# Scores of the gated linear attention by eight levels of block widths, its output mixed tile by tile

## The chip, the cores and the metric

The kernel is one program on one core of a Trainium2 chip. The metric is the device time of one execution in microseconds (us). TensorE (PE) multiplies, and loads its weights beside that (PEld); VectorE (DVE), ScalarE (ACT) and GpSimd (POOL) work elementwise; SyncE (SP) issues the DMAs. PE's clock is granted at one of two levels, 2.4 or 1.2 GHz; the views give it as 1.00 or 0.50.

## The reference

Two decoder layers over 256 positions of width 1024, in float32. Layer 0 is a mix of attention heads and a dense SwiGLU, layer 1 a gated linear attention (GLA) and a mixture of eight experts. The change lies in the GLA:

```python
def gla_mixer(h, w_in, w_a2, b_a, o_norm, w_out):
    q, k, v, r, a1 = _split(h @ w_in, C_SPLITS)          # 4 heads, dk 128, dv 256
    q = q.reshape(B, S, H, dk) * (dk ** -0.5)
    log_a = (jax.nn.log_sigmoid((a1 @ w_a2 + b_a).astype(jnp.float32)) / GLA_TAU).reshape(B, S, H, dk)
    ...
        b = jnp.cumsum(gc, axis=2)
        o_inter = jnp.einsum('bhcd,bhde->bhce', qc * jnp.exp(b), state)
        decay = jnp.where(causal, jnp.exp(jnp.where(causal, dlt, 0.0)), 0.0)   # dlt = b_i - b_j
        att = jnp.einsum('bhid,bhjd,bhijd->bhij', qc, kc, decay)
        o_intra = jnp.einsum('bhij,bhje->bhie', att, vc)
    ...
    o = rmsnorm(o, o_norm).astype(h.dtype).reshape(B, S, GLA_DV) * jax.nn.silu(r)
    return o @ w_out
```

So the score of query i and key j is a sum over 128 channels of q, k and the product of the decays from j+1 to i.

## The kernel before

Activations stand in two tiles of 128 positions (`t`), transposed in `hT_hi` and `hT_lo` (each f32 value as a rounded part and a rest, hence three matmuls per product, `mm3`, L502 to L504). Weights come in a stream of units of 128x2048 (1 MB). SP fetches unit u into one of six `raw` slots once DVE has made the rest of unit u-6. ACT rounds a unit (`split`, L1060: it waits until PE has used unit u-3, `units_used`), DVE makes the rest (L1345), and PE waits for that (`w_lo`). No scheduler is at work: the order of every engine is the order of the code in its block, and semaphores tie the blocks together. Each engine runs its own instructions strictly in that order.

The GLA's stage, from some 372 us to 535 us of the span. The input projection has six column groups `cg` of 8 blocks, two units each: q (0), k (1), v (2, 3) and the output gate r (4, 5).

- PE: `channels(0)` makes q transposed (channels on partitions); L825 makes the decays' logits z; `channels(1)` k; `group` 2, 3, 4; `diagonal(0)` (L840), `group` 5, `cross(0)` (L852, L855), eight dummy matmuls (`keep_busy`), `cross(1)`, `diagonal(1)`, the keys of tile 0 for queries of tile 1 (`far`, L872), the mix of the values (L882, L885), the transposes of the normed output, and the output projection `C_OUT`, tile by tile (`by_tile`), with the second tile's transposes after four blocks of the first tile.
- The scores within a tile come in three kinds. Pairs in one block of 8: DVE makes for each of the 8 offsets the difference of the cumulated logs (L1717), q times k (L1721) and, after ACT's exp (L1197), their product (L1732), and `diagonal` sums over the channels with 8 matmuls of 512 columns against a selecting matrix. Pairs in other blocks of 8 or 32: six copies of k and two of q scaled to block edges (L1694 to L1704, L1775), taken by `cross` in 24 matmuls of 32 or 24 columns per tile. `take_att` (L1740 to L1750) adds the parts, masked, into `att`.
- After the mix, ACT sums squares (L1228), POOL takes the root (L469), DVE multiplies root, output and gate (L1805, `mixed`); the norm's gain was multiplied into the gate before (L1798). `turned` fills `hT_hi` (ACT) and `hT_lo` (DVE) from the transposes; for the output projection it needs no gain, so two instructions per tile and engine (L1069, L1356), while norms with gains take eight (L1075, L1363).

Of the kernel before, what the change touches and what calls it, by code (L numbers as in the profile page):

```python
# [36 lines left out]
P = 128  # L37
# [13 lines left out]
UB = 4  # L51
# [8 lines left out]
GB = 8  # L60
GE = 32
NGE = P // GE
NED = NGE - 1 + GE // GB - 1

# [18 lines left out]
C_ID, C_TRI, C_ONES, C_IOTA, C_BD = 0, 128, 256, 384, 512  # L83
C_BE = 640
C_SEL = 768
C_ROPE = C_SEL + GB + P
# [8 lines left out]
R_QN, R_KN, R_FQ, R_FK, R_ON, R_GB, R_FB = 0, 64, 128, 192, 256, 512, 536  # L95
R_NORM = 544
# [7 lines left out]
def constants():  # L104
# [7 lines left out]
    c[:, C_BD:C_BD + P] = (i[:, None] <= i[None, :]) & (i[:, None] // GB == i[None, :] // GB)  # L112
    c[:, C_BE:C_BE + P] = i[:, None] // GE == i[None, :] // GE

    c[:, C_SEL:C_SEL + GB + P] = np.arange(GB + P)[None, :] % GB == 0
# [37 lines left out]
def trunk(nc, x_d, w_d, const_d, mask_d, small_d, comp_d, wa2_d, out_d):  # L153
    ctx = ExitStack()
    with ctx:
# [49 lines left out]
        mbd = cst[:, C_BD:C_BD + P]  # L205
        mbe = cst[:, C_BE:C_BE + P]
# [51 lines left out]
        gb = cg_(NT * 512).rearrange("p (t n) -> p t n", t=NT)  # L258
        gv = hn
        prod = cg_(GB * 512).rearrange("p (s n) -> p s n", s=GB)  # L260
        kt = cg_(NED * NT * 512).rearrange("p (i t n) -> p i t n", i=NED, t=NT)
        qt = cg_(2 * NT * 512).rearrange("p (i t n) -> p i t n", i=2, t=NT)
        a1T = cg_(SEQ)

        roots, root_diag = esc[:, 0, 0:SEQ], esc[:, 1, 0:SEQ]

        att, atmp = kt[:, 0, :, :], kt[:, 1, :, :]
        gr = kt[:, 2:4, :, :].rearrange("p i t n -> p (i t n)").rearrange("p (t n) -> p t n", t=NT)
        kbar, qbar, far = kt[:, 4, 0, :], kt[:, 5, 0, :], kt[:, 5, 1, :]

        def q_view(i):

            return qt[:, i, :, :].rearrange("p t n -> p (t n)")\
                .rearrange("p (g b r) -> p g b r", b=4, r=(GE, GB)[i])[:, :, 1:4, :]

        def before_edge(a_, i):

            block_, width = (P, (i + 1) * GE) if i < NGE - 1 else (GE, (i - NGE + 2) * GB)
            return a_.rearrange("p (g n) -> p g n", n=block_)[:, :, 0:width]

        def k_view(i):
            return before_edge(kt[:, i, :, :].rearrange("p t n -> p (t n)"), i)


        gz = prod[:, 0:2, :].rearrange("p s n -> p (s n)")
        ge = prod[:, 2:4, :].rearrange("p s n -> p (s n)")
        rmask = prod[:, 4:6, :].rearrange("p s n -> p (s n)")


# [15 lines left out]
        def cf(n):  # L305
# [27 lines left out]
            h2T a1 a1_sb z zb absz soft decay gla_qk gla_vr prod_zero kt_zero diag_arg diag_exp prod diag  # L333
            k_arg k_exp kt q_arg q_exp qt cross att far_arg far_exp far_ops far_psum far_sb gla_o gla_ss
# [5 lines left out]
        def turned_before(g):  # L340

            return sum(NT * NK if j in GAINED else NT * 2 for j in range(g))

# [113 lines left out]
        def _(pool):  # L457
# [26 lines left out]
            pool.wait_ge(S["x_ready"], 4)  # L484
            nc.gpsimd.memset(kt, 0.0).then_inc(S["kt_zero"], 1)
            norm(1)
            norm(2)
            pool.wait_ge(S["decay"], 1)
            nc.gpsimd.memset(prod, 0.0).then_inc(S["prod_zero"], 1)
# [7 lines left out]
        def _(pe):  # L497
# [307 lines left out]

            def channels(cg, b0):

                for k in range(NK):
                    b = cg * NK + k
                    if b == UB:  # L810
                        spread_roots()
                    if b % UB == 0:
                        pe.wait_ge(S["w_lo"], U_C_IN + b // UB + 1)
# [8 lines left out]
            channels(0, 0)  # L822
            pe.wait_ge(S["a1_sb"], 1)
            for h in range(GH):
                last = mm(bank[4 + h // 2][:, h % 2 * SEQ:(h % 2 + 1) * SEQ], wa2[:, h * P:(h + 1) * P], a1T[0:32, :],  # L825
                          start=True, stop=True)
            last.then_inc(S["z"], 1)
            pe.wait_ge(S["zb"], 1)
            channels(1, 4)
            pe.wait_ge(S["gla_qk"], 4)  # L830
            group(U_C_IN, 2, (0, 1))
            group(U_C_IN, 3, (2, 3))
            pe.wait_ge(S["gla_qk"], 8)
            group(U_C_IN, 4, (4, 5))

            def diagonal(t):

                pe.wait_ge(S["prod"], GB * (t + 1))
                for s_ in range(GB):
                    last = mm(bank[t][:, :], cst[:, C_SEL + GB - s_:C_SEL + GB - s_ + P], prod[:, s_, :],  # L840
                              start=(s_ == 0), stop=(s_ == GB - 1))
                last.then_inc(S["diag"], 1)

            def cross(t):
                if t:
                    pe.wait_ge(S["att"], t)
                for h in range(GH):
                    hs = slice(h * P, (h + 1) * P)

                    for i in range(1, NGE):  # L850
                        at = h * P + i * GE
                        mm(bank[2][:, at:at + GE], kt[:, i - 1, t, hs], qt[:, 0, t, at:at + GE], start=True, stop=True)  # L852
# [7 lines left out]

            pe.wait_ge(S["gla_vr"], 4)
            diagonal(0)
            group(U_C_IN, 5, (6, 7))
            pe.wait_ge(S["kt"], 1)
            pe.wait_ge(S["qt"], 1)
            cross(0)
# [1216 lines left out]
```

## Time and profile before

| | us |
|---|---|
| median of 3 runs (lowest, highest) | 1327.59 (1326.4, 1331.55) |
| the profiled execution | 1329.8 |
| its span | 1328.0 |
| PE, DVE, ACT busy in the span | 1288.3, 1036.7, 822.1 |
| the experts' stage, 535 us to the end | 793 |
| the GLA's stage, 372 us to 535 us | 163 |

The last column of a line in the windows is what the DMAs moved; PEclk is the mean granted clock of PE. The chain of work that ended last is followed back from the last instruction, step by step, to what released it: time in it is time that the end depends on. A matmul of float32 data shows as two records.

### The profile page before, as it was taken

How to read it: one execution, taken by the hardware profiler on the slowest of the kernel's cores; microseconds unless marked ns; L12 is line 12 of the kernel's file. 1: busy time of each engine (PE TensorE's matmuls, PEld its weight loads, DVE VectorE, ACT ScalarE, POOL GpSimd, SP SyncE). 2: the span in 40 equal slices, each digit the busy share in tenths (PEclk: the TensorE clock that was granted, in tenths of full speed). 3: DMA queues.
4: the chain of work that ended last, by engine and by line, in shares of the span. 5: the costliest groups of instructions: out<-in, count | busy, mean ns of one | idle time of the engine just before them, and what ended most of it. 6: DMA issues, size and time to landing. Idle time of an engine off the chain costs nothing.

```text
span 1328.0 us, 17323 instructions
## 1 busy us (share of the span) xinstructions
PE 1288.3 (97%) x6142; PEld 1058.1 (80%) x6152; DVE 1036.7 (78%) x1046; ACT 822.1 (62%) x895; POOL 33.1 (2%) x29
## 2 busy tenths in 40 slices
PE   6999999999999999999999999999999999999997
PEld 5877888888888766788888888888888888888885
DVE  4786664455468846789989989989989989989985
ACT  6435364444454535677777777777777777777773
POOL 0130010000001010000000000000000000000000
PEclk9999999999989989999999999999999999999999
DMA  9640045454434302699999989989999999999991
GB/s 375 240 142 18 1 164 188 187 185 185 181 148 158 127 32 95 257 350 366 359 341 362 364 337 366 353 341 363 355 343 360 353 342 356 355 347 372 349 373 74
DMA packets 48793, 350.72 MB, mean 264 GB/s; under 512 B 5424, under 2 KB 5552, under 8 KB 6480
## 3 DMA queue, kind: packets, MB, share of 16 engines
q1 hardware_dynamic: 48720, 349.67, 69.9%
q8 instruction: 55, 0.90, 0.3%
q14 instruction: 18, 0.15, 0.0%
HBM read 348.60 MB, written 1.05 MB: 263 GB/s over the span
## 4 chain that ended last, share of the span: by engine, by line
PE 93%; DVE 4%; ACT 1%; issue 1%; POOL 1%; DMA 1%; SPq 0%; DVEq 0%; ACTq 0%
PE bank L502 27%; PE bank L504 26%; PE bank L503 26%; PE bank L968 1%; PE bank L691 1%; PE bank L717 1%; PE bank L840 1%; DVE wlo L1345 1%; PE bank L699 1%; PE bank L919 1%; PE bank L920 1%; ACT whi L1060 1%; DMA raw<-in_weights 1%; PE bank L855 1%; PE bank L942 1%
## 5 line engine op out<-in xcount | busy, mean ns | idle before, releaser
L1925 DVE TENSOR_TENSOR wlo<-raw,whi 128x2048 fp32r<-128x2048 f32 x261 | 597.1, 2290 | 77.4 <-ACT whi L1272 74.6
L1272 ACT CAST whi<-raw 128x2048 fp32r<-128x2048 f32 x261 | 499.3, 1913 | 135.8 <-PE bank L504 135.7
L502 PE MATMUL bank<-whi,hT_hi 128*128 128x512 f32 (+1 forms) x1104 | 432.0, 391 | 13.2 <-DVE wlo L1345 7.7
L504 PE MATMUL bank<-whi,hT_lo 128*128 128x512 f32 (+1 forms) x1104 | 429.9, 389 | 0.0
L503 PE MATMUL bank<-wlo,hT_hi 128*128 128x512 f32 (+1 forms) x1104 | 429.7, 389 | 0.0
L502 PEld LDWEIGHTS bank<-whi,hT_hi 128*128 128x128 f32 x1104 | 208.1, 188 | 58.1 <-issue 10.0
L504 PEld LDWEIGHTS bank<-whi,hT_lo 128*128 128x128 f32 x1104 | 208.2, 189 | 43.0
L503 PEld LDWEIGHTS bank<-wlo,hT_hi 128*128 128x128 f32 x1104 | 208.3, 189 | 42.3 <-issue 0.2
L1345 DVE TENSOR_TENSOR wlo<-raw,whi 128x2048 fp32r<-128x2048 f32 x68 | 155.6, 2290 | 103.0 <-ACT whi L1060 102.3
L1060 ACT CAST whi<-raw 128x2048 fp32r<-128x2048 f32 x68 | 129.9, 1912 | 117.1 <-PE bank L504 114.8
L502 PE MATMUL bank<-whi,h_hi 128*128 128x512 f32 x440 | 180.1, 409 | 0.0
L504 PE MATMUL bank<-whi,h_lo 128*128 128x512 f32 x440 | 172.7, 392 | 0.0
L503 PE MATMUL bank<-wlo,h_hi 128*128 128x512 f32 x440 | 172.5, 392 | 0.0
L504 PEld LDWEIGHTS bank<-whi,h_lo 128*128 128x128 f32 x440 | 83.0, 189 | 18.2
L503 PEld LDWEIGHTS bank<-wlo,h_hi 128*128 128x128 f32 x440 | 83.4, 190 | 14.9
L502 PEld LDWEIGHTS bank<-whi,h_hi 128*128 128x128 f32 x440 | 83.0, 189 | 14.8
L1290 ACT ACTIVATE sg<-bank 128x256 f32<-128x256 f32 x88 | 33.9, 385 | 67.1 <-PE bank L504 67.1
L1930 DVE TENSOR_TENSOR h_lo<-bank,h_hi 128x256 fp32r<-128x256 f32 x88 | 36.7, 417 | 1.0 <-ACT h_hi L1276 1.0
L1151 ACT ACTIVATE sg<-bank,rstd 128x256 f32<-128x256 f32 x22 | 10.4, 473 | 42.1 <-PE bank L504 42.0
L1945 DVE TENSOR_TENSOR hact<-sg,bank 128x256 f32<-128x256 f32 x88 | 36.4, 414 | 0.0
L968 PE MATMUL bank<-cst,hact 128*128 128x128 f32 x176 | 33.5, 271 | 2.1 <-DVE h_lo L1930 2.1
L968 PEld LDWEIGHTS bank<-cst,hact 128*128 128x128 f32 x176 | 24.4, 139 | 13.8 <-issue 2.5
(290 smaller groups left out, 971.9 us busy)
## 6 DMA issues: line engine op xcount, KB each, us to landing
raw<-in_weights SPq DMA_DIRECT2D x329, 1024.0 KB, 5.1
arena<-in_compress SPq DMA_DIRECT2D x1, 1088.0 KB, 14.6
x<-in_x SPq DMA_DIRECT2D x2, 512.0 KB, 5.8
out<-x SPq DMA_DIRECT2D x2, 512.0 KB, 3.6
cst<-in_constants SPq DMA_DIRECT2D x1, 604.0 KB, 11.3
sml<-in_small SPq DMA_DIRECT2D x1, 402.0 KB, 5.3
msk_bits<-in_masks SPq DMA_DIRECT2D x1, 288.0 KB, 14.4
cst<-in_constants SPq DMA_DIRECT2D x1, 64.0 KB, 3.1
```

The source lines that it names most:

```text
L502: mm(out_, a_hi, b_hi, start=start, stop=False)
L503: mm(out_, a_hi, b_lo, start=False, stop=False)
L504: return mm(out_, a_lo, b_hi, start=False, stop=stop)
L691: last = mm(b[:, j * kw:(j + 1) * kw], q, k, start=False, stop=(j == n - 1))
L968: last = nc.tensor.transpose(bank[2][:, j * P:(j + 1) * P], hact[:, (par + c) % 2, j * P:(j + 1) * P], ident)
L1060: nc.scalar.copy(whi[:, u % SPLIT, :, :], raw[:, u % RAW, :, :]).then_inc(S["w_hi"], 1)
L1272: nc.scalar.copy(whi[:, u % SPLIT, :, :], raw[:, u % RAW, :, :]).then_inc(S["w_hi"], 1)
L1290: A(sg[:, (par + c) % 2, :], bank[(par + c) % 2][:, 0:CH], ACT.Silu).then_inc(S["m_silu"], 1)
L1345: V.tensor_tensor(wlo[:, u % SPLIT, :, :], raw[:, u % RAW, :, :], whi[:, u % SPLIT, :, :].bitcast(F32), ALU.subtract).then_inc(S["w_lo"], 1)
L1925: V.tensor_tensor(wlo[:, u % SPLIT, :, :], raw[:, u % RAW, :, :], whi[:, u % SPLIT, :, :].bitcast(F32), ALU.subtract).then_inc(S["w_lo"], 1)
L1930: V.tensor_tensor(h2_lo[:, (par + c) % 2, :], bank[2][:, 0:CH], h2_hi[:, (par + c) % 2, :].bitcast(F32), ALU.subtract).then_inc(S["m_h2T"], 1)
L1945: V.tensor_tensor(hact[:, (par + c) % 2, :], sg[:, (par + c) % 2, :], bank[(par + c) % 2][:, CH:2 * CH], ALU.mult).then_inc(S["m_hact"], 1)
```

## The change

The sum over channels is done by PE for all pairs, in levels. At level l (block width w = 2^l), the queries of every odd block of width w meet the keys of the even block just before it. The query copy of a level carries the product of the decays from its block's start up to it, the key copy that of the decays behind it up to its block's end. `level_up(l)` makes level l from level l-1: odd halves of q and even halves of k are multiplied by the neighbour block's total (L1729, L1731 of the changed kernel), and the totals are multiplied in pairs (L1734); ACT copies the other halves (`level_copy`). `take(l)` puts a level's scores into `att` with a predicated copy under a mask (level 6 with a plain copy of 64 partitions). The pairs i = j come from a product of q and k with no decay (`same_key`), and the eighth level is `far`. The decays themselves come from one exp of the logs; running sums, block-edge copies, POOL's two large memsets and the dummy matmuls are gone.

On the input side, z moves into the middle of `channels(0)`, and ACT takes the bias and the absolute value over from DVE. On the output side, the scores are finished before cg 5: the values are mixed first, then cg 5 runs tile by tile, and the transposes of tile 0 stand in its last quarter. The output goes to its own tile `gm`; the gain of its norm moves from the gate into `turned(4, ...)`, which so takes the form with eight instructions. Two constants tables shrink, the small inputs from 804 to 550 columns.

```diff
-            channels(0, 0)
-            pe.wait_ge(S["a1_sb"], 1)
-            for h in range(GH):
...
-            pe.wait_ge(S["gla_vr"], 4)
-            diagonal(0)
-            group(U_C_IN, 5, (6, 7))
...
-            cross(0)
-            keep_busy(8, 1)
-            cross(1)
-            diagonal(1)
+            def level(l):
+
+                pe.wait_ge(S["lev"], l + 1)
+                if l:
+                    pe.wait_ge(S["lev_copy"], l)
+                if l >= 2:
+                    pe.wait_ge(S["lev_taken"], l - 1)
+                b = bank[LEVEL_BANKS[l]]
+                for m in range(NT * GH):
+                    last = mm(b[:, m * 64:(m + 1) * 64].rearrange("p (b w) -> p b w", w=1 << l),
+                              level_k(l)[:, m * P:(m + 1) * P], block_of(level_q(l)[:, m * P:(m + 1) * P], l, 1),
+                              start=True, stop=True)
+                last.then_inc(S["lev_psum"], 1)
...
+            channels(0, 0)
+            pe.wait_ge(S["zb"], GH)
+            channels(1, 4)
+            pe.wait_ge(S["gla_qk"], 4)
+            group_with(U_C_IN, 2, (0, 1), first_levels)
+            level(1)
+            group_with(U_C_IN, 3, (2, 3), lambda: level(2))
+            level(3)
+            level(4)
+            pe.wait_ge(S["gla_vr"], 2)
+            group_with(U_C_IN, 4, (0, 1), lambda: level(5))
+            level(6)
+            far_keys()
+            pe.wait_ge(S["gla_vr"], 4)
+            pe.wait_ge(S["lev_taken"], NLEV + 2)
+            mix_values(0)
+            mix_values(1)
+            by_tile(U_C_IN, 5, (2, 3), None, (1, 4),
+                    lambda: transposes(gm, 4, 0, lambda half: pe.wait_ge(S["mixed"], 2 * (half + 1))))
             by_tile(U_C_OUT, 0, C_OUT_BANKS[0], 4, (0, 4),
-                    lambda: transposes(hn, 4, 1, lambda half: pe.wait_ge(S["mixed"], GH + 2 * (half + 1))))
+                    lambda: transposes(gm, 4, 1, lambda half: pe.wait_ge(S["mixed"], GH + 2 * (half + 1))))
...
+            level_copy(6)
+            far_copy()
+            split(U_C_IN + 11)
+            vr(4)
...
+            split(U_C_IN + 12)
+            square_sums(0)
+            square_sums(1)
+            vr(5, 0)
             turned(4, 0)
+            split(U_C_IN + 13)
+            vr(5, 1)
             turned(4, 1)
...
+                V.tensor_tensor(block_of(level_q(l), l - 1, 1), block_of(level_q(l - 1), l - 1, 1), totals(l - 1, 0),
+                                ALU.mult)
+                V.tensor_tensor(block_of(level_k(l), l - 1, 0), block_of(level_k(l - 1), l - 1, 0), totals(l - 1, 1),
+                                ALU.mult).then_inc(S["lev"], 1)
...
+            def take(l):
...
+                V.copy_predicated(dst, bc(mask, 1, NT * GH), src).then_inc(S["lev_taken"], 1)
...
-GAINED = {0: 0, 2: 1, 3: 2, 5: 3}
+GAINED = {0: 0, 2: 1, 3: 2, 4: None, 5: 3}
```

Where PE leaves the scores in the kernel before, at the mix's end and the output projection (L512 transposes the mixed output, L502 to L504 multiply; a wait's semaphore stands in brackets):

```order
L882 MATMUL bank4<-hn,arena 128x256
L885 MATMUL bank4<-hn,arena 128x256
L512 MATMUL bank0<-cst,hn 128x128 [waits mixed]
...
L512 MATMUL bank1<-cst,hn 128x128 [waits mixed]
...
L502 MATMUL bank5<-whi,hT_hi 128x512 [waits w_lo,hT]
```

and in the changed kernel, where L868 and L871 mix, L509 transposes, L499 to L501 multiply, and banks 2 and 3 belong to cg 5:

```order
L847 MATMUL bank4<-arena 128x64 [waits lev_taken,lev_copy,lev]
L859 MATMUL bank5<-arena 128x128 [waits lev_taken,lev_copy,lev]
L868 MATMUL bank6<-hn,arena 128x256 [waits lev_taken,gla_vr]
...
L871 MATMUL bank5<-hn,arena 128x256
L499 MATMUL bank2<-whi,hT_hi 128x512 [waits w_lo]
...
L509 MATMUL bank0<-cst,arena 128x128 [waits mixed]
...
L509 MATMUL bank1<-cst,arena 128x128 [waits mixed]
...
L499 MATMUL bank6<-whi,hT_hi 128x512 [waits w_lo,hT]
```

Between the mix and the transposes there now stand 36 matmuls of cg 5, and 12 more between these and the first matmul that needs their result.

DVE in the changed kernel from the last levels to the mixed output (L1755 is the predicated copy, L1391 makes a unit's rest, L1764 is `mixed`):

```order
L1755 COPY_PREDICATED arena<-cst,bank7 128x16x32 [waits lev_taken,lev_psum]
L1729 TENSOR_TENSOR arena<-arena 128x16x32 [waits dve_chain,lev_psum,lev_copy,lev]
...
L1391 TENSOR_TENSOR wlo<-raw,whi 128x2048 [waits w_hi]
L1752 COPY arena<-bank4 64x8x64 [waits lev_taken,lev_psum]
...
L1764 SCALAR_TENSOR_TENSOR arena<-bank6,ors,arena 128x256 [waits gla_vr,gla_rstd]
...
L1764 SCALAR_TENSOR_TENSOR arena<-bank4,ors,arena 128x256 [waits gla_vr,gla_rstd]
...
L1391 TENSOR_TENSOR wlo<-raw,whi 128x2048 [waits w_hi]
```

The last row but one and the last stand in this order: the rest of the second unit of `C_OUT` is made between the first and the second half of tile 1's mixed output.

## Rows read from the trace of the kernel before

**Rows 1.** The page: span and instructions; busy time and share of the engines.

```profile
span 1328.0 us, 17323 instructions
PE 1288.3 (97%) x6142; PEld 1058.1 (80%) x6152; DVE 1036.7 (78%) x1046; ACT 822.1 (62%) x895; POOL 33.1 (2%) x29
```

**Rows 2.** Windows: stretch, its length, busy us (instructions) by engine, PEclk, DMA.

```profile
386.40:402.40 16.00, 14.25 (x97) 14.22 (x97) 9.11 (x9) 6.68 (x6) 0.00 (x0) 0.79 0.25 98
484.50:494.50 10.00, 6.81 (x29) 5.34 (x30) 4.09 (x10) 2.37 (x7) 1.21 (x2) 0.83 0.00 0
494.50:535.20 40.70, 36.15 (x174) 25.71 (x175) 27.59 (x65) 20.53 (x34) 0.89 (x2) 0.96 0.27 103
```

**Rows 3.** The chain in order of time, 435 to 495: start, us in it, what.

```profile
435.28 6.87 PE bank L840 x16
...
453.04 0.59 PE bank L852 x6
...
460.75 0.85 PE bank L852 x6
...
469.64 8.54 PE bank L840 x16
478.18 0.89 PE bank L872 x8
...
484.46 0.26 issue
...
489.00 0.50 PE bank L502
...
493.61 0.87 PE bank L512 x8
```

**Rows 4.** PE in order of time: start, us busy, what, idle time before it.

```profile
384.44 1.99 PE L825 MATMUL bank<-arena,wa 32*128 32x256 f32 x8
388.18 0.58 PE L502 MATMUL bank<-hT_hi,whi 128*128 128x256 f32 x1 [1.75 <-DVE arena L1660]
...
402.44 0.40 PE L502 MATMUL bank<-whi,hT_hi 128*128 128x512 f32 x1
```

**Rows 5.** PE in layer 0's attention, in order of time, as in rows 4.

```profile
113.83 1.00 PE L717 MATMUL bank<-arena 128*128 128x64 f32 x8
114.67 0.38 PE L684 MATMUL bank<-msk_bits 128*128 128x512 bf16 x1
```

**Rows 6.** Windows, as in rows 2: layer 0's attention, two stretches at half clock.

```profile
106.00:154.00 48.00, 47.31 (x326) 39.42 (x331) 35.02 (x74) 21.06 (x96) 0.00 (x0) 1.00 0.00 1
388.20:394.20 6.00, 6.00 (x28) 6.00 (x29) 3.95 (x3) 1.96 (x2) 0.00 (x0) 0.50 0.38 153
462.80:472.80 10.00, 10.00 (x37) 8.14 (x37) 4.60 (x8) 5.25 (x8) 0.00 (x0) 0.50 0.29 107
```

**Rows 7.** Groups by line and shape, 366 to 520: busy us, mean ns; idle before.

```profile
L1345 DVE TENSOR_TENSOR wlo<-raw,whi 128x2048 fp32r<-128x2048 f32 x17 | 38.9, 2288 | 18.3 <-ACT whi L1060 18.1 <-DVE arena L1647 0.2
L1060 ACT CAST whi<-raw 128x2048 fp32r<-128x2048 f32 x16 | 30.6, 1911 | 21.6 <-PE bank L504 21.6
...
L1075 ACT ACTIVATE hT_hi<-bank,sml 128x128 fp32r<-128x128 f32 x32 | 8.6, 399 | 9.0 <-PE bank L512 9.0
...
L1805 DVE SCALAR_TENSOR_TENSOR hn<-bank,ors,arena 128x256 f32<-128x256 f32 x8 | 3.3, 477 | 2.2 <-POOL ors L469 2.2
...
L1647 DVE SCALAR_TENSOR_TENSOR arena<-bank,esc 128x256 f32<-128x256 f32 x8 | 2.8, 413 | 0.1
...
L1740 DVE TENSOR_TENSOR arena<-bank,cst 128x512 f32<-128x512 f32 x2 | 1.4, 691 | 10.7 <-PE bank L840 9.5 <-PE bank L855 1.3
L1721 DVE TENSOR_TENSOR arena<-arena 128x512 f32<-128x512 f32 x2 | 1.4, 684 | 0.0
...
L1173 ACT ACT_TABLE_LOAD x1 | 1.3, 1283 | 0.0
...
L1173 ACT ACTIVATE arena<-arena 128x1024 f32<-128x1024 f32 x1 | 1.1, 1059 | 4.4 <-DVE arena L1667 4.4
```

More of the change, by code:

```diff
@@ L804, in spread_roots, with decays @@
                 last.then_inc(S["roots_psum"], 1)
+            def decays():
+                pe.wait_ge(S["a1_sb"], 1)
+                for h in range(GH):
+                    last = mm(bank[4 + h // 2][:, h % 2 * SEQ:(h % 2 + 1) * SEQ], wa2[:, h * P:(h + 1) * P],
+                              a1T[0:32, :], start=True, stop=True)
+                last.then_inc(S["z"], 1)
             def channels(cg, b0):
@@ L832, in _ @@
[L832 to L846, printed above, removed]
-                for h in range(GH):
[L848 to L852, printed above, removed]
-                    for j in range(1, GE // GB):
-                        inner = slice(j * GB, (j + 1) * GB)
-                        last = mm(bank[3][:, hs].rearrange("p (b r) -> p b r", r=GE)[:, :, inner],
-                                  kt[:, NGE - 2 + j, t, hs],
-                                  qt[:, 1, t, hs].rearrange("p (b r) -> p b r", r=GE)[:, :, inner],
-                                  start=True, stop=True)
-                last.then_inc(S["cross"], 1)
@@ L874, in _, with same_key @@
-            last.then_inc(S["far_psum"], 1)
-            pe.wait_ge(S["gla_vr"], 8)
-            for t in range(NT):
-                pe.wait_ge(S["att"], t + 1)
+            def same_key():
+                pe.wait_ge(S["gla_qk"], 8)
+                for t in range(NT):
+                    for h in range(GH):
+                        c = slice(h * P, (h + 1) * P)
+                        last = mm(bank[4 + t][:, c], gk[:, t, c], gq[:, t, c], start=True, stop=True)
+                    last.then_inc(S["lev_psum"], 1)
@@ L1175, in _, with vr @@
             A(ge, ge, ACT.Ln, bias=1.0).then_inc(S["soft"], 1)
+            split(U_C_IN + 4)
+            act.wait_ge(S["logd"], 1)
+            A(ga, gz, ACT.Exp, scale=1.0 / 16.0).then_inc(S["decay"], 1)
             split(U_C_IN + 5)
             split(U_C_IN + 6)
-            def vr(cg):
-                act.wait_ge(S["units_used"], U_C_IN + 2 * (cg + 1))
+            def vr(cg, only=None):
                 half = cg % 2
-                for t in range(NT):
+                for t in range(NT) if only is None else (only,):
+                    if cg == 5 and t == 0:
+                        act.wait_ge(S["tile0"], 4)
+                    else:
+                        act.wait_ge(S["units_used"], U_C_IN + 2 * (cg + 1))
@@ L1189, in _ @@
+            level_copy(1)
             split(U_C_IN + 7)
+            level_copy(2)
+            vr(2)
+            level_copy(3)
             split(U_C_IN + 8)
[L1191 to L1199 removed]
@@ new lines, in _ @@
+            level_up(0)
+            split(U_C_IN + 6)
+            level_up(1)
+            take_same()
+            take(0)
+            split(U_C_IN + 7)
+            level_up(2)
+            take(1)
+            level_up(3)
+            split(U_C_IN + 8)
+            take(2)
+            level_up(4)
+            split(U_C_IN + 9)
+            take(3)
+            take(4)
+            level_up(5)
+            split(U_C_IN + 10)
+            take(5)
+            level_up(6)
+            level_up(7)
```

399 lines of the change are left out of this document (165 added, 234 removed).

## The prediction

> **What bounds the kernel now.** The page first: PE is busy 97% of the span [rows 1], so only PE's own work, its waits and its clock can be worth time, and DVE and ACT matter where PE waits for them. Then the windows, stretch by stretch: the experts' stage after 535 is untouched by the change, so the question is the GLA's stage. There the windows show PE away from full use three times: the clock at 0.79 after 386.4, and 6.81 us busy in the 10 us after 484.5 at 0.83 [rows 2]; in between it is busy, but with scores. The chain in order of time shows that nearly all of this is PE's own work, so what PE does less ends the kernel earlier, as long as the two other engines keep up [rows 3]. The profiled execution took 1329.8 us (span 1328.0 and 1.8 around it), 2.2 us above the median of 1327.59; what I take off, I take off the median.
>
> **Removed from PE, or no longer waited for.** All on the path.
> 1. The wait before the second channel group: z starts at 384.44 and its chain ends 1.75 us before 388.18, where DVE releases PE [rows 4]. In the changed kernel z is issued a quarter of a group earlier, and 24 matmuls cover the bias that ACT now adds: 1.75 off.
> 2. That wait is followed by six us at half clock [rows 6]. The group of 96 matmuls took 402.44 - 388.18 = 14.26 us [rows 4]. The group before it, at full clock, started at 372.4 and ended at 384.44 with 0.45 us of another product inside, so 11.6. Without the fall: 2.65 off.
> 3. `diagonal(0)`: 6.87 [rows 3].
> 4. `cross(0)`, the dummies and the wait for `att`: 460.75 - 453.04 = 7.71 [rows 3].
> 5. `cross(1)`: 469.64 - 460.75 = 8.89, most of it at half clock [rows 3, 6].
> 6. `diagonal(1)`: 8.54 [rows 3].
> 7. The gap from the end of the mix to the output projection, 489.00 - 484.46 = 4.54 [rows 3]: squares, root, product, transposes, copies. The transposes stay (0.87, as those of the second tile [rows 3]), the rest goes behind cg 5: 3.67 off.
> 8. The 12 matmuls after this gap took 493.61 - 489.00 = 4.61 [rows 3]; the three groups of 48 from 402.44 to 435.28 [rows 3, 4] give 0.228 each, so 12 cost 2.74 at full clock: 1.87 off.
>
> Sum: 1.75 + 2.65 + 6.87 + 7.71 + 8.89 + 8.54 + 3.67 + 1.87 = 41.95 us.
>
> **Added to PE.** `same_key` has 8 products of 128 columns: `far` has four and takes 0.89 [rows 3], so 1.78. Each of seven levels has 8 products (16 records) of 64 columns. The trace has this shape: eight records of L717 start at 113.83 and the next instruction at 114.67 [rows 5], 0.105 a record, 1.68 a level. The cross products give 0.59 for six records and `far` 0.111 a record [rows 3], so a narrow f32 product costs the same whether it has 32, 64 or 128 columns. I take the dearer 0.111: 1.78 a level, 12.5 for seven. The bounds: 11.8, and twice 12.5 if all ran at half clock. Added without new waits: 14.25 us. `far` and the mix are as before.
>
> **Do DVE and ACT keep up?** The prices: a rest 2.29 (2.2 from start to start), a rounding 1.91, a pass over 1024 elements 1.06 on ACT, a table load 1.28, 128x512 on DVE 0.69, from PSUM (L1740) as from SBUF (L1721), the scaling of four banks four times some 0.35 [rows 7]. With PE's clock as the measure (z ends 386.4, channels 398.0, first half of cg 2 403.5), I walked the three queues:
> - z is there at 383.5 now. ACT: biases 1.2, absolute value 1.1, load, exp, load, log 4.7, rounding of unit 4 to 392.7. DVE: rest to 395.0 (PE needs it at 398.0), the log decay 1.2. ACT: exp 1.1 to 397.4, rounding of unit 5 to 399.4. DVE: rest to 401.7, k scaled to 403.2. PE asks for k at 403.5. **The thinnest cover, 0.3 us**; behind that wait stand `same_key`, level 0 and all later PE work. If ACT is 1 us later, PE waits 0.7.
> - Level l+1 needs two products of 0.6 and a total on DVE after level l, and two copies on ACT. Between levels PE has 24 matmuls (5.5 us) at most places; levels 3 and 4, and 6 and `far`, come in pairs, but both members are made before. DVE has 25.8 us of work (six rests 13.2, `level_up` some 10.8, the diagonal and level 6 1.8) and six predicated copies between 403.2 and 445.9. The predicated copy isn't in the trace. Bounds: 0.6, as for any 128x512 there, and 1.2 if the mask counts as a pass of its own; nothing is gained below 0.6. I take 0.7; both ends are hidden. The last take must be over when `far` is, at 445.9: on this walk ACT's copies of the far operands end at 440.9, the rounding of unit 11 at 442.8, its rest at 445.0, the last copy at 445.6. Covered.
> - The mix ends at 451.3, tile 0 of cg 5 at 456.8, and the transposes of tile 0 come at 459.5. Squares, root, product (0.48 each [rows 7]) and the gate of tile 0 are done at 458.4. Covered, and what was the gap of item 7 costs nothing.
> - `turned(4, t)` now takes eight instructions per engine. On ACT eight of them take some 2.2 us (L1075 busy 8.6 in 32 [rows 7]) against 1.2. The 12 matmuls left of cg 5 cover the first half.
> - At the second tile's transposes a new wait stands. Behind the rest of unit 13 (rounded from 462.3, since ACT first does `turned(4, 0)`; rest done 466.5) DVE queues the second half of tile 1's product, 0.8 us. PE asks at 466.3 and gets it at 467.4: **1.05 us added**, and in that queue everything of the output projection waits.
>
> **Sum.** 14.25 + 1.05 - 41.95 = -26.65 us. The smaller inputs table (254 columns of 128 floats, 130 KB) lies ahead of the first weights and may give 0.3 more. 1327.6 - 26.65 = 1300.9; I say **1301 us**. The tail from 494.5 to 535.2 [rows 2] starts that much earlier and is otherwise the same, and so are the experts.
>
> **Rivals.**
> - *A new clock fall.* The clock went to half after the wait of 1.75 us, and again inside `cross(1)`, among narrow products [rows 3, 4, 6]. Such a fall lasts six to ten us, and costs half of that, so one costs 3 to 5 us: 1304 to 1306, two 1309. Against it: layer 0's attention has products of a level's shape [rows 5] and small gaps, and its 48 us run at 1.00 [rows 6], and here 5.5 us of full-width matmuls stand between the levels. The likeliest place is the wait of 1.05 us. The Trainium skill, "TensorE: Matmul & The Clock Gate" (A second HAM failure mode: psum-queue depth-cycling), says that many micro-idles between groups of matmuls, as banks are cycled, make the clock swing between its levels; by that rule, with the levels in four banks in turn, these would run at half clock for good. Worked from rows: levels, `same_key` and `far` then cost twice their 15 us, and the matmuls between them partly too, some 20 us more, 1321. The attention stretch, which cycles banks as well, speaks against it [rows 6]: 3%.
> - *ACT or DVE later than walked.* Strided copies or the predicated one cost up to double, or every handoff 0.1 us more; then k comes late, the wait at the transposes grows, and 2 to 6 us come back: 1303 to 1307.
> - *Slower than before, by one mechanism:* the predicated copy with broadcast mask runs far slower than DVE's other passes. DVE has 42.7 us for 25.8 us and six copies; it becomes the bound from 2.8 us a copy, and all 26.65 us are lost from (16.9 + 26.65) / 6 = 7.3 us a copy, ten times any 128x512 in the trace [rows 7]. At 9 us: 1338.
> - *More than forecast:* a level costs 1.68 (0.7 less), the wait at the transposes vanishes (1.05), the tail's own loss (clock 0.96, [rows 2]) falls away with other timing (up to 1.6): 1298.
>
> **How the numbers follow.** Forecast with all waits as walked, 1299 to 1303: 0.58. A new clock fall: 0.17 and 0.03 for the lasting one. ACT or DVE late: 0.12. More: 0.07. Slower: 0.03. The range reaches from 1297.5 to 1307, which leaves out the lasting fall, the copy, and the ends of two others, some 0.15. A measurement of this kernel can tell 0.5% (6.6 us) from no change; under 1321 is faster: 0.95. Same 0.02, slower 0.03.
>
> **What would show it.** Right: the stage from the start of the channels to the experts lasts some 137 us; a level takes 1.7 to 1.8 us of PE; no PE wait for zb, gla_qk or lev above 0.5 us; one wait of about 1 us at L509 for the mixed output; the predicated copies near 0.7 us; PEclk 1.00 from 386 to the output projection. Wrong: a window there at 0.50, a predicated copy above 2 us, or a PE wait before `same_key` or before L868 of more than 1 us.

## The result, and the profile after

| | before | changed |
|---|---|---|
| median, us (lowest, highest) | 1327.43 (1326.4, 1331.55) | 1307.99 (1306.28, 1309.29) |
| ratio to before, 95% interval | | 0.9849 [0.9832, 0.9866] |
| the profiled execution | 1329.8 | 1308.1 |

The change makes the kernel 1.5% faster. The forecast was 1301 with a range from 1297.5 to 1307, so the time lies 7 us above the forecast and 1 us above the range. The page of the changed kernel, against [rows 1]:

```profile
span 1306.2 us, 17280 instructions
PE 1271.1 (97%) x6144; PEld 1046.0 (80%) x6144; DVE 1011.7 (77%) x1002; ACT 822.0 (63%) x901; POOL 24.0 (2%) x27
```

To find where the time went, cut each span at the same three events: the first matmul of the first channel group, the first matmul behind the second tile's transposes (the end of the GLA's stage), and the first matmul of the experts. Windows of before, columns as in [rows 2]:

```profile
372.40:494.48 122.08, 116.29 (x594) 95.60 (x594) 85.87 (x122) 55.15 (x76) 8.82 (x7) 0.92 0.33 121
494.48:535.17 40.69, 36.14 (x173) 25.71 (x174) 27.56 (x65) 20.55 (x34) 0.89 (x2) 0.96 0.27 103
535.17:1328.00 792.83, 783.14 (x3568) 644.51 (x3568) 702.48 (x553) 573.32 (x498) 0.00 (x0) 1.00 0.90 339
```

and of the changed kernel:

```profile
372.10:467.55 95.45, 94.61 (x586) 84.63 (x585) 56.96 (x72) 53.29 (x78) 4.99 (x6) 1.00 0.38 134
467.55:508.20 40.65, 34.91 (x179) 24.78 (x177) 30.61 (x72) 22.83 (x37) 0.89 (x2) 1.00 0.42 150
508.20:1306.20 798.00, 787.89 (x3568) 644.47 (x3568) 703.25 (x553) 573.16 (x498) 0.00 (x0) 1.00 0.89 337
```

The GLA's stage, the only one that the change is about, is 122.08 - 95.45 = 26.63 us shorter; the sum said 26.65. It starts 0.3 us earlier. The tail, the second row, takes the same time. But the experts' stage, whose code is untouched, has the same 3568 records, the clock at 1.00 in both and nearly the same idle time on TensorE (9.7 and 10.1 us), and takes 798.00 - 792.83 = 5.17 us more. 26.63 + 0.30 + 0.04 - 5.17 = 21.8, the difference of the spans.

Which instructions are slower? Groups by line and shape of TensorE in 750 us of the experts (columns as in [rows 7]), before:

```profile
L503 PE MATMUL bank<-wlo,hT_hi 128*128 128x512 f32 x682 | 265.3, 389 | 0.0
L503 PE MATMUL bank<-wlo,h_hi 128*128 128x512 f32 x333 | 130.0, 390 | 0.0
L504 PE MATMUL bank<-whi,h_lo 128*128 128x512 f32 x332 | 129.8, 391 | 0.0
```

and changed:

```profile
L500 PE MATMUL bank<-wlo,hT_hi 128*128 128x512 f32 x667 | 259.7, 389 | 0.0
L500 PE MATMUL bank<-wlo,h_hi 128*128 128x512 f32 x337 | 133.3, 396 | 0.0
L501 PE MATMUL bank<-whi,h_lo 128*128 128x512 f32 x337 | 133.3, 396 | 0.0
```

The products of the gathered tokens (`hT`) take the same 389 ns; those of the hidden activations (`h2_hi`, `h2_lo`, which the trace names h_hi and h_lo) take 5 to 6 ns more each in these groups. The busy time of one overlaps the next, so what counts is the distance from start to start. One block of them, first and twelfth row, in order of time, before:

```profile
704.11 0.39 PE L503 MATMUL bank<-wlo,h_hi 128*128 128x512 f32 x1
...
706.63 0.39 PE L502 MATMUL bank<-whi,hT_hi 128*128 128x512 f32 x1
```

and changed:

```profile
678.04 0.39 PE L500 MATMUL bank<-wlo,h_hi 128*128 128x512 f32 x1
...
680.61 0.40 PE L499 MATMUL bank<-whi,hT_hi 128*128 128x512 f32 x1
```

That is 2.52 / 11 = 229 ns against 2.57 / 11 = 234 ns. Over all such rows of the stage the means are some 228.7 and 233.2 ns; about a thousand of them make 4.3 to 4.8 us of the 5.17, and the rest lies in the stage's other rows. No instruction of the change stands there. What the change does do there is in its last sentence: two tables become smaller. `cst` loses 8 columns and `sml` 254, 262 columns of 4 bytes or 1048 bytes per partition; with the allocator's rounding to 32 bytes, the arena and every tile placed behind it start 1056 bytes lower. `whi`, `wlo`, `hT_hi` and `hT_lo` lie ahead of the tables and stay.

### The profile page after: what moved, and what is told of

Same layout as the page of the kernel before. It is cut to its first block, busy times and chain, and to the rows that moved or that the text cites. A ratio compares the mean times of both kernels' runs of the same rounds, so it can differ in the third digit from the quotient of the medians.

```text
span 1306.2 us, 17280 instructions
## 1 busy us (share of the span) xinstructions
PE 1271.1 (97%) x6144; PEld 1046.0 (80%) x6144; DVE 1011.7 (77%) x1002; ACT 822.0 (63%) x901; POOL 24.0 (2%) x27
## 3 DMA queue, kind: packets, MB, share of 16 engines
HBM read 348.47 MB, written 1.05 MB: 268 GB/s over the span
## 4 chain that ended last, share of the span: by engine, by line
PE 92%; DVE 4%; ACT 2%; issue 1%; POOL 1%; DMA 0%; SPq 0%; DVEq 0%; ACTq 0%
PE bank L499 27%; PE bank L501 27%; PE bank L500 27%; PE bank L992 1%; PE bank L688 1%; PE bank L714 1%; DVE wlo L1391 1%; PE bank L847 1%; PE bank L696 1%; ACT whi L1084 1%; PE bank L509 1%; PE bank L966 1%; PE bank L968 1%; PE bank L651 1%; PE bank L944 0%
## 5 line engine op out<-in xcount | busy, mean ns | idle before, releaser
L1318 ACT CAST whi<-raw 128x2048 fp32r<-128x2048 f32 x261 | 499.0, 1912 | 140.6 <-PE bank L501 140.2
L499 PE MATMUL bank<-whi,hT_hi 128*128 128x512 f32 (+1 forms) x1104 | 432.0, 391 | 9.8 <-DVE wlo L1391 7.0
L501 PE MATMUL bank<-whi,hT_lo 128*128 128x512 f32 (+1 forms) x1104 | 429.6, 389 | 0.0
L499 PEld LDWEIGHTS bank<-whi,hT_hi 128*128 128x128 f32 x1104 | 207.7, 188 | 54.6 <-issue 8.9
L501 PEld LDWEIGHTS bank<-whi,hT_lo 128*128 128x128 f32 x1104 | 207.6, 188 | 43.1
L1391 DVE TENSOR_TENSOR wlo<-raw,whi 128x2048 fp32r<-128x2048 f32 x68 | 155.7, 2291 | 100.3 <-ACT whi L1084 99.3
L499 PE MATMUL bank<-whi,h_hi 128*128 128x512 f32 x440 | 181.8, 413 | 0.0
L501 PE MATMUL bank<-whi,h_lo 128*128 128x512 f32 x440 | 174.4, 396 | 0.0
L501 PEld LDWEIGHTS bank<-whi,h_lo 128*128 128x128 f32 x440 | 82.9, 188 | 20.0
L499 PEld LDWEIGHTS bank<-whi,h_hi 128*128 128x128 f32 x440 | 83.1, 189 | 16.2
L1099 ACT ACTIVATE hT_hi<-bank,sml 128x128 fp32r<-128x128 f32 x80 | 21.7, 387 | 25.6 <-PE bank L509 25.6
L1409 DVE SCALAR_TENSOR_TENSOR hT_lo<-bank,sml,hT_hi 128x128 fp32r<-128x128 f32 x80 | 21.6, 344 | 20.7 <-ACT hT_hi L1099 20.7
```

The source lines that it names most:

```text
L499: mm(out_, a_hi, b_hi, start=start, stop=False)
L501: return mm(out_, a_lo, b_hi, start=False, stop=stop)
L1099: A(hT_hi[:, k, cols], src[:, j * P:(j + 1) * P], ACT.Copy, scale=sml[:, gc:gc + 1])\
L1318: nc.scalar.copy(whi[:, u % SPLIT, :, :], raw[:, u % RAW, :, :]).then_inc(S["w_hi"], 1)
L1391: V.tensor_tensor(wlo[:, u % SPLIT, :, :], raw[:, u % RAW, :, :], whi[:, u % SPLIT, :, :].bitcast(F32), ALU.subtract).then_inc(S["w_lo"], 1)
L1409: V.scalar_tensor_tensor(hT_lo[:, k, cols], src[:, j * P:(j + 1) * P], sml[:, gc:gc + 1], hT_hi[:, k, cols].bitcast(F32), ALU.mult, ALU.su ...
```

## Experiments on the experts' stage

Below, the rest of a tile is the distance from the start of `whi` to its own start in SBUF, in bytes of one partition, modulo 256. For `h2_hi` and `h2_lo` it is 0 in the kernel before and 224 in the changed one; for `hT_hi` and `hT_lo` it is 0 in both.

**Realign the changed kernel.**

```diff
-        ctx.enter_context(nc.sbuf_tensor("line_pad", [P, 8], F32))
+        ctx.enter_context(nc.sbuf_tensor("line_pad", [P, 16], F32))
```

> The changed kernel with 32 bytes per partition more of padding ahead of the arena, nothing else; the bases of the arena, h2_hi and h2_lo are multiples of 64 bytes again, as in the kernel before. Placement theory: in the trace of the changed kernel the matmuls whose stationary tile is h2_hi or h2_lo stand 233.4 ns apart, in that of the kernel before 228.7, and 1056 of them in the experts make some 5 us. So they come back to 228 to 230 ns, the experts' stage to 792 to 793.5 us (798.0 in the changed kernel), and the time to some 1302.5 us, ratio to the kernel before 0.981. Rival (the experts are slower for the timing of the weight stream or for the clock, not for the address): 233 ns, 798 us, 1308 us, ratio 0.985.

Measured: 1302.96 us, ratio 0.9805 [0.9780, 0.9831], experts' stage 793.5 us, h2's products 228.6 ns from start to start. These are the numbers that the placement predicts.

**Shift the kernel before**: the same edit in it, which takes h2 out of line there.

> The kernel before with 32 bytes per partition more of padding, nothing else; h2_hi and h2_lo now start 32 bytes behind a multiple of 64. Placement theory: the matmuls with h2 as stationary tile go from 228.7 to 233.4 ns, experts' stage 793 to 798 us, the layer 0 feed-forward 1 us longer, time 1327.5 + 5.5 = 1333 us, ratio 1.004. Rival: unchanged, 1327.5, ratio 1.000.

Measured: 1334.79 us, ratio 1.0045 [1.0028, 1.0062], experts' stage 797.1 us. Its groups:

```profile
L504 PE MATMUL bank<-whi,h_lo 128*128 128x512 f32 x331 | 131.2, 396 | 0.0
L503 PE MATMUL bank<-wlo,h_hi 128*128 128x512 f32 x331 | 130.9, 396 | 0.0
```

So in the kernel before, 32 bytes of padding with no other edit bring h2's products to 396 ns and cost 6 us by the ratio, of which the trace has 4.2 in the experts' stage.

**Shift h2 alone.**

```diff
+        h_pad = sb("h_pad", [P, 8])
         h2_hi = sb("h2_hi", [P, 2, CH], F32R)
         h2_lo = sb("h2_lo", [P, 2, CH], F32R)
+        h_pad2 = sb("h_pad2", [P, 8])
```

> The kernel before with only h2_hi and h2_lo moved by 32 bytes; the arena, the gate tiles, and all that lies behind keep multiples of 64. If the stationary operand's own address is the cause: 233 ns for its matmuls and 1333 us, ratio 1.004, as with everything shifted. If another of the moved tiles is the cause (the arena, the gate's tiles, the gather's): 228.7 ns and 1327.5 us, ratio 1.000.

Measured: 1333.84 us, ratio 1.0037 [1.0020, 1.0055], experts' stage 796.8 us. Here the arena and all tiles ahead of `h2_hi` keep their places; those behind `h2_lo` move by 64 bytes, and these products read none of them. So it is h2, not another of the tiles that the change moved.

**Shift hT, or the weights.** The changed kernel as realigned, with pads of 8 columns around `hT_hi` and `hT_lo`, or around `whi` and `wlo`.

> The changed kernel with aligned placement (1303.0 us), but hT_hi and hT_lo (stationary tile in two of three expert matmuls and in all of the projections of tokens, moving operand in the channel groups) start 32 bytes behind a multiple of 64; everything else stands on multiples of 64. If 64 bytes matter for any stationary tile of 128 columns: 4.7 ns for each of some 2800 matmuls (226.8 to 231.5 ns in the experts), 13 us: 1316 us, ratio 0.990. Rival (it matters for h2 alone, because these are written and read in quick turn, or the matmuls of hT have other limits): 1303 us, ratio 0.9805.

> The changed kernel with aligned placement (1303.0 us), but whi and wlo start 32 bytes behind a multiple of 64, everything else on multiples of 64. They are the moving operand in all large matmuls except the two channel groups, where they are stationary (192 matmuls of 256 columns). If only the stationary tile's address counts: some 1 us more, 1304 us. If the moving operand's address counts as well: 3000 matmuls by 5 ns or more, 1318 us or above.

Measured: 1325.89 us, ratio 0.9981 [0.9962, 1.0000], and 1325.61 us, ratio 0.9984 [0.9965, 1.0003]. Either edit costs 23 to 24 us by the ratios and takes back nearly all that the change brings. Groups of the experts with hT shifted, and then with the weights shifted:

```profile
L502 PE MATMUL bank<-wlo,hT_hi 128*128 128x512 f32 x660 | 260.9, 395 | 0.0
L503 PE MATMUL bank<-whi,h_lo 128*128 128x512 f32 x332 | 131.0, 395 | 0.0
```

```profile
L502 PE MATMUL bank<-wlo,hT_hi 128*128 128x512 f32 x660 | 261.0, 395 | 0.0
L503 PE MATMUL bank<-whi,h_lo 128*128 128x512 f32 x332 | 131.4, 396 | 0.0
```

Now hT's products are slow too: from start to start 233.3 ns, against 226.7 in the realigned kernel, in layer 0's feed-forward as in the experts. I had expected 13 us, or 1 to 15, and two things were left out. I took 4.7 ns for each product of hT, as for h2, and it loses 6.6. And both runs also put h2 on a nonzero rest (64 and 32), so h2's products are slow again. With hT shifted the experts' stage takes 810.1 us against 793.5, with 12.9 us more between the starts of hT's products, 4.7 more between those of h2's and 1.1 less in its other rows; the first channel matmul comes 4.8 us later, and from there to the experts it is 1.0 us more: 22.3 us, the difference of the two spans. The next runs show why the starts of h2, multiples of 64 bytes, didn't keep it fast.

**Own address or distance?** All tiles of the realigned kernel moved together, by a pad of 8 or of 16 columns ahead of the first tile.

> The changed kernel with aligned placement (1303.0 us), every tile of the program moved by 32 bytes together, so that all distances between tiles stay as they are. If each operand's own address counts: all large matmuls at 233 ns as in the two runs with hT or the weights moved, 1325 us or more, ratio 0.998. If only the distance between the stationary and the moving operand counts (0 modulo 64 in the fast kernels): 228.7 and 226.8 ns as in the aligned one, 1303 us, ratio 0.981.

> The same with 64 bytes: all large tiles start at a multiple of 64 that is no multiple of 128. If the own address counts in steps of 64: 1303 us. If it counts in steps of 128: above 1310 us. If only the distance between the operands counts: 1303 us.

Measured: 1303.25 us, ratio 0.9812 [0.9788, 0.9837], and 1301.39 us, ratio 0.9795 [0.9770, 0.9820]. Groups with everything shifted by 32 bytes:

```profile
L501 PE MATMUL bank<-wlo,hT_hi 128*128 128x512 f32 x666 | 259.1, 389 | 0.0
L502 PE MATMUL bank<-whi,h_lo 128*128 128x512 f32 x344 | 134.5, 391 | 0.0
```

Every tile that the large matmuls read starts 32 bytes off its place in the realigned kernel, and all of them are as fast as there; 32 bytes on one of them alone made its products slow. It is the distance between tiles that counts, not the address.

**What step?** The realigned kernel with the padding ahead of the arena at 0, 32, 48, 80 and 144 columns; the last four were executed once each.

> The changed kernel with the padding ahead of the arena left out: h2_hi and h2_lo stand at a multiple of 64 bytes that is no multiple of 128, other than in the kernel before and the aligned one, where they are on multiples of 128. If 64 is the step: 228.7 ns for h2's matmuls, 1303 us, ratio 0.981. If 128 is the step: 233 ns and 1308 us, ratio 0.985.

> The aligned kernel with the padding ahead of the arena 64 bytes larger: h2_hi and h2_lo at 64 modulo 128, as in the run without padding, where h2's matmuls stood 229 to 232 ns apart and the experts' stage took 796.6 us against 791.3 to 793.5 in the kernels with h2 on multiples of 128. If 64 modulo 128 costs something: 795 to 798 us again. If that run was disturbed: 791 to 794 us.

> The aligned kernel with the padding 128 bytes larger: h2 on another multiple of 128. Experts' stage 791 to 794 us and 228.7 ns if multiples of 128 are what counts; more if a larger step counts or if the exact distance to the weights does.

> The aligned kernel with 256 bytes more ahead of the arena, so that the distance from whi to h2_hi, divided by 512 bytes, leaves 256. In the runs so far h2's matmuls were fast where that rest is 0 (228.7 ns; experts' stage 791.3 to 793.5 us) and slower at 32, 64, 128, 448 and 480 (229.6 to 233.5 ns; 796.6 to 798.9 us). If 512 bytes is the step: 231 to 234 ns and 796 to 799 us. If it is 256: 228.7 ns and 791 to 794 us.

> The same with 512 bytes more, rest 0 again and all that follows 512 bytes further on. If 512 bytes is the step: 228.7 ns, experts' stage 791 to 794 us, some 1302 us in all. If the step is larger, or the additional padding itself costs: 796 to 799 us.

| h2's rest (run) | mean ns, `whi,h_lo` | experts' stage, us | time, us |
|---|---|---|---|
| 0 (before) | 391 | 792.8 | 1327.4 |
| 0 (realigned; all shifted by 32; by 64) | 392; 391; 392 | 793.5; 791.9; 793.3 | 1303.0; 1303.3; 1301.4 |
| 0, 256 bytes further | 391 | 792.1 | 1302.4 |
| 0, 512 bytes further | 391 | 792.2 | 1302.5 |
| 64 | 395 | 797.3 | 1307.7 |
| 128 | 395 | 798.9 | 1309.3 |
| 192 (no padding) | 394 | 796.6 | 1305.7 |
| 224 (changed kernel) | 396 | 798.0 | 1308.0 |
| 32 (before, shifted) | 396 | 797.1 | 1334.8 |
| 32 (before, h2 alone) | 395 | 796.8 | 1333.8 |

The step is 256 bytes: every rest of 0 is fast, every other one tried is slow. The single executions suffice for that, since the traces with a rest of 0 have an experts' stage of 791.3 to 793.5 us, and those with h2 off it and hT on it one of 796.6 to 798.9. At 192 the loss was smaller in part of the products (`wlo,h_hi` stayed at 390 ns), which I can't explain. Two things stay open. The matmuls read only the stationary tile and the weights, so the weights are the likely partner; but `raw`, which ScalarE and VectorE read all the while, kept its distance to the weights in all runs but the one that moved them, and no run separates these two. And no trace shows what in the memory does it.

The Trainium skill, "SBUF — State Buffer" (Operand start alignment), says that an operand must start at a multiple of its element size, and that this is "about legality, not speed". All kernels here keep that rule, and their times differ by 23 us.

## Experiments on the stage itself

The places in the changed kernel's trace that the prediction names, TensorE in order of time as in [rows 4]:

```profile
381.25 1.99 PE L807 MATMUL bank<-arena,wa 32*128 32x256 f32 x8
383.17 0.39 PE L499 MATMUL bank<-hT_hi,whi 128*128 128x256 f32 x1
...
403.14 1.95 PE L835 MATMUL bank<-arena 128*128 128x128 f32 x16
404.93 1.34 PE L847 MATMUL bank<-arena 128*128 128x64 f32 x11
...
443.12 1.89 PE L847 MATMUL bank<-arena 128*128 128x64 f32 x16
444.85 1.11 PE L859 MATMUL bank<-arena 128*128 128x128 f32 x8
...
459.34 1.03 PE L509 MATMUL bank<-cst,arena 128*128 128x128 f32 x8
...
467.14 0.66 PE L509 MATMUL bank<-cst,arena 128*128 128x128 f32 x4 [0.84 <-DVE arena L1764]
```

The group goes on behind z (L807) without a wait; `same_key` takes 404.93 - 403.14 = 1.79 us, a level 444.85 - 443.12 = 1.73; the one wait of TensorE in the stage is 0.84 us at the second tile's transposes.

**z back behind the first channel group.**

```diff
-                    if b == UB + 2:
-                        decays()
...
             channels(0, 0)
+            decays()
             pe.wait_ge(S["zb"], GH)
```

> The changed kernel with the decays' logits z moved back from inside the first channel group to behind it, as in the kernel before; the rest of the change stays. By the prediction's items 1 and 2: PE waits some 1.8 to 3 us for the bias before the second channel group (ACT now adds it, after what it has queued), and a stretch at half clock follows that costs 2.65 us: 1308 + 4.4 to 5.6 = 1312.5 to 1313.5 us. Rival (the clock falls for another reason than the wait): only the wait is lost, some 1310 us. Second rival (the chain from z through the log decay to the scaled keys becomes late as well): PE waits at same_key for up to 2 us more, up to 1316 us.

Measured: 1312.44 us, ratio 0.9876 [0.9853, 0.9899], 3.6 us over the changed kernel by the ratios. Their intervals overlap (0.9853 to 0.9866), so the trace decides: from the first channel matmul to the first of the gather (L943) it has 131.4 us against 128.15. The wait and the stretch after it:

```profile
389.14 0.39 PE L499 MATMUL bank<-hT_hi,whi 128*128 128x256 f32 x1 [1.66 <-ACT arena L1196]
```

```profile
390.50:394.30 3.80, 3.80 (x21) 3.80 (x21) 0.00 (x0) 3.76 (x4) 0.00 (x0) 0.55 0.02 4
```

1.66 us of waiting, and 3.8 us at a clock of 0.55, which cost 1.7. So both items stand as mechanisms; the fall lasts 3.8 us here and lasted six in the kernel before [rows 6], and its price goes with that.

**The levels twice.** `for m in 2 * list(range(NT * GH))` in `level`: each level's products are made twice.

> The changed kernel with aligned placement (1303.0 us), every level's 8 products made twice into the same place. Theory (TensorE's own work sets the time all through the stage): seven times 1.73 us more, 12.1 us: 1315.1 us, ratio 0.9895. Rival (the other two engines are as late as TensorE, so that part of the added work only fills waits): clearly less than 12 us, 1308 to 1312 us.

Measured: 1315.33 us, ratio 0.9900 [0.9847, 0.9952]. From the first channel matmul to the gather the trace has 140.6 us against 128.05 in the realigned kernel: 12.5 us, against seven times 1.73. Nothing of the added work disappears in waits, so TensorE's own work sets the time wherever a level stands.

**The predicated copies four times.** Each `copy_predicated` is repeated three times before it signals. VectorE in the changed kernel, the first three copies:

```profile
409.12 1.32 DVE L1755 COPY_PREDICATED arena<-cst,bank 128x512 f32<-128x512 uint32 x1
...
414.14 1.34 DVE L1755 COPY_PREDICATED arena<-cst,bank 128x512 f32<-128x512 uint32 x1
...
421.42 0.71 DVE L1755 COPY_PREDICATED arena<-cst,bank 128x512 f32<-128x512 uint32 x1 [2.35 <-PE bank L847]
```

> The changed kernel with aligned placement (1303.0 us), every predicated copy made four times. They take 1.32 and 1.34 us at block widths 1 and 2 and some 0.72 at the four others, 5.54 us in all; so 16.6 us more for VectorE, and some 2 us for the handoffs. The prediction gave VectorE 42.7 us for 25.8 us of other work: 25.8 + 22.2 + 2 = 50 us, 7 us late: 1310 us, ratio 0.986. Rival (the cover is thinner than the sum over the stretch says, since each rest must be ready at its own time): up to 18 us late, 1321 us, and a stretch at half clock on top.

Measured: 1307.85 us, ratio 0.9849 [0.9809, 0.9890]. From the first channel matmul to the gather: 134.9 us against 128.05, 6.8 us, where 7 were expected. TensorE's waits in it, and the stretch behind the first:

```profile
PE bank L847 <- DVE arena L1731: 2.4, 1, 2.4
...
PE bank L868 <- DVE arena L1754: 1.8, 1, 1.8
```

```profile
430.00:436.00 6.00, 6.00 (x28) 5.12 (x29) 5.79 (x7) 4.05 (x5) 0.00 (x0) 0.72 0.45 162
```

The two waits make 4.2 us, and the clock of 0.72 over six us costs 1.7 more, so part of the delay is again a clock fall behind a wait. The prediction's point from which VectorE becomes the bound, 2.8 us a copy, fits: six copies of 3.7 us on average give a delay, six of 0.9 give none. No run stands between these two.

**The output side put back.** In the realigned kernel cg 5 comes first, then the mix, then the transposes of tile 0; ScalarE and VectorE take unit 13 ahead of squares and product.

```diff
+            by_tile(U_C_IN, 5, (2, 3))
             mix_values(0)
             mix_values(1)
-            by_tile(U_C_IN, 5, (2, 3), None, (1, 4),
-                    lambda: transposes(gm, 4, 0, lambda half: pe.wait_ge(S["mixed"], 2 * (half + 1))))
+            transposes(gm, 4, 0, lambda half: pe.wait_ge(S["mixed"], 2 * (half + 1)))
```

> The changed kernel with aligned placement (1303.0 us), its output side put back: cg 5 first, then the mix, then squares, root, product and the transposes of tile 0 with nothing beside them on TensorE; ScalarE and VectorE take unit 13 ahead of the squares. By the prediction's items 7 and 8 a gap of 3.67 us and a stretch at half clock of 1.87 us return, and the wait of 0.86 us at the second tile's transposes goes: 1303.0 + 5.5 - 0.9 = 1307.6 us, ratio 0.984. Rival (the gap is filled by other work or the clock stays up): 1305 to 1306.5 us.

Measured: 1303.75 us, ratio 0.9817 [0.9770, 0.9863]; channels to gather 128.7 us against 128.05. The interval of the ratio reaches from 1297 to 1309 us and would allow either expectation; the stage in the trace shows that both were too high. Of the gap only this is left:

```profile
461.81 1.36 PE L509 MATMUL bank<-cst,arena 128*128 128x128 f32 x8
464.31 0.50 PE L499 MATMUL bank<-whi,hT_hi 128*128 128x512 f32 x1 [1.14 <-DVE hT_lo L1409]
```

Why was it 2.54 us in the kernel before? TensorE and VectorE there:

```profile
489.00 0.50 PE L502 MATMUL bank<-whi,hT_hi 128*128 128x512 f32 x1 [2.54 <-DVE hT_lo L1356]
```

```profile
486.69 1.66 DVE L1805 SCALAR_TENSOR_TENSOR hn<-bank,ors,arena 128x256 f32<-128x256 f32 x4 [0.94 <-POOL ors L469]
488.26 1.28 DVE L1356 TENSOR_TENSOR hT_lo<-bank,hT_hi 128x512 fp32r<-128x512 f32 x2
```

VectorE makes tile 1's mixed output before tile 0's `hT_lo`, though it has to wait for tile 1's root first; in the changed kernel, and in this one, `hT_lo` comes first. So the last experiment changes that order alone, in the kernel before:

```diff
                  .then_inc(S["mixed"], 1)
-            turned(4, 0)
+                if i == GH - 1:
+                    turned(4, 0)
             turned(4, 1)
```

> The kernel before with one change of order on VectorE: it makes hT_lo of tile 0 (two instructions) before the mixed output of tile 1 (four), not behind it. In the trace of the kernel before, hT_hi is there at 486.3 and 487.1, VectorE waits at 486.69 for tile 1's root, then multiplies for 1.66 us, and hT_lo comes only at 488.3; TensorE waits 2.54 us for it up to 489.00 and then runs at half clock. If this order makes most of the gap (items 7 and 8): first matmul of the output projection at some 487.0, 2 us earlier, and with the clock not falling 1.87 more: 2 to 3.9 us, 1327.5 to 1324.5, ratio 0.997 to 0.9985. Rival (the gap needs the mix to be moved, as in the changed kernel): no change, 1.000.

Measured: 1324.62 us, ratio 0.9966 [0.9947, 0.9985]. TensorE, and VectorE:

```profile
487.84 0.50 PE L502 MATMUL bank<-whi,hT_hi 128*128 128x512 f32 x1 [0.62 <-DVE hT_lo L1356]
...
490.69 1.03 PE L512 MATMUL bank<-cst,hn 128*128 128x128 f32 x8
```

```profile
487.09 1.48 DVE L1356 TENSOR_TENSOR hT_lo<-bank,hT_hi 128x512 fp32r<-128x512 f32 x2 [0.58 <-ACT hT_hi L1069]
488.48 1.65 DVE L1805 SCALAR_TENSOR_TENSOR hn<-bank,ors,arena 128x256 f32<-128x256 f32 x4
```

The wait falls from 2.54 to 0.62 us, and the 12 matmuls after it take 490.69 - 487.84 = 2.85 us, at full clock. In the kernel before they took 4.44, from 489.00 to the transposes' start at 493.44 in the same view; the chain's row at 493.61, which the prediction used, lies 0.17 inside the transposes. Together 1.92 + 1.59 = 3.5 of the 5.54 us that I had put on moving the mix come from the order of two steps on VectorE. The ratio gives 4.5 us, with an interval from 2 to 7; the profiled execution has channels to gather only 2.1 us shorter, because its clock stood at half just as long in all, 20.5 us, though at another place: among the scores, and behind neither the wait for z nor this one.

## Why the prediction was wrong, step by step

- **Items 1 and 2, z:** right in kind. Wait and clock fall are gone, and return when z is put back, at 3.4 us in that run against the 4.4 taken. The 2.65 of item 2 is the price in one execution, though: the same wait of 1.75 us stands in four traces with the code of the kernel before, and behind it the clock is at half for 6.8 us (before), 3.4 (before shifted), 3.4 (h2 alone) and not at all (`hT_lo` first).
- **Items 3 to 6, the old scores:** right; their 32 us are gone from TensorE.
- **Items 7 and 8, the gap behind the mix:** the size is right but for 0.17 us of item 8, the cause only in part. Some two thirds (3.5 of 5.54 us) belong to VectorE's order, which the change also altered and which the prediction didn't look at.
- **Added work:** `same_key` 1.79 us (1.78 predicted), a level 1.73 (1.78). Right.
- **Thin cover for k:** predicted 0.3 us, no wait in the trace. The predicated copy was taken as 0.7 with bounds of 0.6 and 1.2: it took 0.71 from width 4 on, but 1.32 and 1.34 at widths 1 and 2, above the upper bound, and all were hidden. The wait at the second tile's transposes: 1.05 predicted, 0.84 found.
- **The sum of the stage:** 26.65 predicted, 26.63 found. That the two agree to 0.02 us is luck. The terms named above are off by 0.2 us and more, and the stage of the kernel before isn't that steady: channels to gather took 154.5 us in its trace, 152.5 in the shifted one and 155.1 in the one with h2 alone shifted, with TensorE at half clock for 20.5, 17.0 and 23.9 us of it. The changed kernel took 128.0 to 128.2 us in all nine traces that leave this stage and the distance of hT to the weights as they are.
- **The rivals:** the GLA's stage and the tail have a clock of 1.00, so there was no new clock fall; ScalarE and VectorE were on time. The rule of the Trainium skill, "TensorE: Matmul & The Clock Gate" (A second HAM failure mode: psum-queue depth-cycling), that micro-idles between groups make the clock swing, doesn't show in this trace.
- **The step that failed** is the last one of the sum: the tail "is otherwise the same, and so are the experts". The experts, 61% of the span, are not: 5.17 us more, of which the realigned kernel gives back 4.5, because the smaller tables moved h2 off the 256-byte step to the weights. The tail has the same length (40.65 against 40.69 us), but by two effects that cancel, as the rows below show. With the placement restored the ratio is 0.9805, which on 1327.4 is 1301.5 us, half a microsecond from the forecast. I had counted the smaller table as 0.3 us of transfer and nothing else; that the span before held a tile named `line_pad` just ahead of the arena was in the code to be seen.

Near the end of the tail TensorE waits for VectorE, before and changed:

```profile
531.91 0.52 PE L931 MATMUL bank<-cst,hn 128*128 128x128 f32 x3 [0.88 <-DVE esc L1895]
```

```profile
504.94 0.63 PE L955 MATMUL bank<-cst,hn 128*128 128x128 f32 x4 [2.16 <-DVE esc L1883]
```

The stretch of half clock in the tail (0.96, [rows 2]) did go, which the prediction held to be worth up to 1.6 us. It was worth nothing: TensorE finished earlier and waited 1.28 us longer at this place.

The realigned changed kernel, 0.9805 of the time before, beats both kernels; the edit is one number.

## What to carry to other kernels

When a change alters the size of any statically placed tile, list what lies behind it and compare its distance to the operands it is read with, modulo 256 bytes here, before and after; a stage that no edit touches can pay for it, and a pad of a few columns gives it back. Before crediting a restructuring with a gap that it closes, look at the order in which the releasing engine does its work: a swap of two steps may have closed it. And in a stage bound by one engine a plain sum of its instructions, at their prices in the trace, forecast a reordering of 120 us more closely than the stage's own variation of 2.6 us between executions of the old code; it was the part called unchanged that had to be priced.

## What the runs showed of the hardware that I had not expected

- A 128x512 matmul with a stationary tile of 128x128 follows the next at 226.7 to 227.7 ns (hT, in the feed-forward and in the experts) or 228.7 (h2), if that tile and the weights are a multiple of 256 bytes apart, and at 232 to 233.5 if not (230 at a rest of 192). Moving everything together, `raw` included, by 32 or 64 bytes changes nothing.
- The predicated copy of 128x512 costs 1.33 us when the mask's and target's inner runs are 1 or 2 elements, and 0.71 to 0.73 us from 4 elements on, from the same PSUM banks; VectorE's other passes of 128x512 in the levels take 0.67 to 0.72 at every width.
- An f32 product of 128x64 costs 0.108 us a record and one of 128x128 0.112: the number of columns hardly counts at this size.
- The same wait of TensorE can bring the clock down or not: 1.75 us before the second channel group were followed by 6.8, 3.4, 3.4 and 0 us at half clock in four traces with the same code there. One trace doesn't give the price of such a fall.
